# The seven passages between sub-layers: a panel's split in four pieces, and the first chunk's high part made by VectorE from the scaled stream

## Chip, cores and metric

One Trainium2 chip, one core, one launch. The metric is the time of the launch on the device in microseconds, lower is better. TensorE (PE), VectorE (DVE), ScalarE (ACT), GpSimd (POOL) and SyncE's DMA queue (SP) run their own instruction streams and wait for each other through semaphores.

## What is computed

272 tokens (16 meta tokens and 256) of width 1024 pass through eight sub-layers: FFN, neighbourhood attention, FFN, FFN, differential attention, FFN, a mixer of block attention and mLSTM, and an MLP. Each is

```
h = h + c * rmsnorm(f(rmsnorm(h, g_in)), g_post)      # f: projections, attention, swiglu or relu^2
rmsnorm(x, g) = x * rsqrt(mean(x*x) + 1e-6) * g
```

From the fifth sub-layer on, 256 tokens are carried. All weights are fp32.

## The kernel before

**Layout.** The stream `h` lies in SBUF with the width on the partitions: 8 chunks `h[:, c, :]` of 128 rows by 272 (later 256) tokens. Sub-layer k (0 to 7) is phases n = 2k (into it) and 2k+1 (out of it). `NA, DA, MIX, MLP` are k = 1, 4, 6, 7.

**Split products.** Every fp32 product is made of three: high by high, high by low, low by high. A panel of weights, 1024 rows by 256 columns (128x2048 in SBUF), comes by DMA into `raw`, ACT rounds it to `w_hi` (`high`, L1400), DVE makes `w_lo = raw - w_hi` (`low`, L1856). Four slots are used in turn. The activations are split in the same way: ACT makes `x_hi[c] = h[c] * gain[c]` (`high_part`, L1463), DVE `x_lo[c]` (`low_part`, L1867). The factor rsqrt of the norm is not in them. It is applied to the products later, so that they need not wait for it.

**A passage** is the way from sub-layer k to k+1, k = 0 to 6. What stands below as passage k is this:

1. `last_panel`: PE makes the two halves (m = 0, 1) of the last output bank one after the other; ACT squares each (`square_half`, L1429).
2. `sum_rest`: PE sums the squares over the partitions with matmuls against ones: L925 (earlier squares), at k = 0, 2, 3, 5 L928 (half 0), and L932 (half 1). Then eight small matmuls by `keep_warm` (L941) fill PE's time. At k = 1, 4, 6 half 0 has been added by DVE before, and L928 is left out.
3. `deviation`: ACT makes `sd` (L1443) and `floor` (L1446) from the sum. The stream is carried scaled: with it `h*sd + y` is the new stream, where `y` are the scaled outputs (`scaled_y`, L1890).
4. `residual`: DVE, chunk by chunk: `scale_h` (L1896, h*sd), `add_y` (L1902, + y), and between them `low_part`. ACT makes `x_hi` of each chunk when it is added.
5. `first_panels`: PE takes the first two panels of the next phase together, chunk by chunk (`shared_chunk`): 8 matmuls with `x_hi` of the chunk (L709), then 4 with `x_lo` (L715). It waits for each chunk's `x_hi` and `x_lo`.

At k = 0, 2, 3, 5 (after an FFN) both panels' `low` stand on DVE's stream ahead of `residual`, and both panels' `high` on ACT's stream ahead of the square of half 0. At k = 1, 4, 6 the same holds, with smaller phases before them. GpSimd adds squares of the output (L2702, L2707) and has nothing to do in the passage itself.

The orders of all engines are written out by hand; no planner is used.

Of the kernel before, what the change touches and what calls it, by code (L numbers as in the profile page):

```python
# [135 lines left out]
def program(nc, A, out):  # L136

    with ExitStack() as ctx:
# [34 lines left out]
        ones = sb("ones", [P, P])  # L173
        eps = sb("eps", [P, 2])
# [61 lines left out]
        c = [end]  # L236
        line = sb("line", [8, 2 * NT - 1 - NM], F32, c)
        assert c[0] <= nc.sbuf_usable_end
# [78 lines left out]
        w_lo_ready = sem("w_lo_ready")  # L317
        panel_used = sem("panel_used")
# [10 lines left out]
        sum_ready = sem("sum_ready")  # L329
        sd_ready = sem("sd_ready")  # L330
# [171 lines left out]
        def mixer_count(k):  # L502

            return (NA, DA, MIX).index(k)
# [20 lines left out]
        def _(sp):  # L525
# [50 lines left out]
            def between(n, panel):  # L576
# [4 lines left out]
                if n == 5:  # L581

                    if panel == 0:
                        sp.wait_ge(line_full, 16)
                        sp.wait_ge(h_ready, DC * (NA + 2))
                    if panel < 8:
                        da_bias_in(panel)
                if n == 11 and panel == 0:

                    sp.wait_ge(h_ready, DC * (DA + 2))  # L590
                    for dst, src in ((causal[:, :], A["causal"]), (causal_t[:, :], A["causal_t"]),
                                     (rotate[:, :], A["rotate"]), (pick[:, :], A["pick"]), (freq[:, :], A["freq"]),
                                     (pos_i[:, :], A["positions_2"][0].partition_broadcast(P)),
                                     (tail[:, :, :], rows(A["w_in_2"][0])[:, :, 3072:3080])):
                        sp.dma_start(dst, src).then_inc(mix_full, 16)

            for n, ph in enumerate(PHASES):
                bodies = ph.panels // 4
                first = 0
                if n == 2 * MLP + 1:  # L600
                    sp.wait_ge(h_ready, DC * (MIX + 2))
# [42 lines left out]
        def _(pe):  # L644
# [44 lines left out]
            def first_panels(k_, tokens):  # L689
# [3 lines left out]
                for k in range(DC):  # L693
                    shared_chunk(n, SPLIT_IN[k_], tokens, k)

            def shared_chunk(n, base, tokens, k):

                    ph = PHASES[n]
                    pe.wait_ge(x_hi_ready, base + k + 1)
                    for j in range(2):  # L700
                        if k == 0:
                            pe.wait_ge(w_lo_ready, ph.p0 + j + 1)
# [3 lines left out]
                        for m in range(2):  # L706
                            w = slice(k * CW + m * P, k * CW + m * P + P)
                            for part in (w_hi, w_lo):
                                nc.tensor.matmul(banks(n, 0, j)[:, m, 0:tokens], part[:, (ph.p0 + j) % SLOTS, w],  # L709
                                                 x_hi[:, k, 0:tokens], start=k == 0 and part is w_hi, stop=False)  # L710
                    pe.wait_ge(x_ready, base + k + 1)
# [207 lines left out]
            def sum_rest(k_, tokens):  # L919

                if k_ in (NA, DA, MIX):
                    pe.wait_ge(post_summed, mixer_count(k_) + 1)
                pe.wait_ge(sq_added, additions(2 * k_ + 1) + 3)
                pe.wait_ge(sd_ready, 2 * k_ + 1)
                nc.tensor.matmul(ps_post[:, 0:tokens], ones[:, :], sq_sum[:, 0, 0:tokens], start=True, stop=False)  # L925
                if k_ not in (NA, DA, MIX):
                    pe.wait_ge(sq_ready, squares_before(2 * k_ + 1) + 4)
                    nc.tensor.matmul(ps_post[:, 0:tokens], ones[:, :], sq[:, 1, 0, 0:tokens], start=False, stop=False)  # L928
# [5 lines left out]
                if k_ < MLP:  # L934
                    keep_warm(aux[:, 0, :], 8)
# [452 lines left out]
        def _(act):  # L1388
# [70 lines left out]
            def high_part(k, c):  # L1459

                g0, _, _, tokens, _ = SUBS[k]
                act.wait_ge(h_ready, DC * k + c + 1)
# [13 lines left out]

            def boundary(k):

                tokens = SUBS[k][4]
                square_half(k, 0)  # L1480
                square_half(k, 1)
                deviation(k, tokens)
                n = 2 * k + 2
# [28 lines left out]
            def output_steps(n, k):  # L1512
# [5 lines left out]
                def step(i, j):  # L1518
# [10 lines left out]
                    if local == last - 2 and k < MLP:  # L1529
                        high(n, i, j + 3)  # L1530
                        if k not in (NA, DA, MIX):
                            high(n, i, j + 4)
# [313 lines left out]
        def _(dve):  # L1846
# [51 lines left out]
            def add_y(k, c0, c1):  # L1898

                tokens = SUBS[k][4]  # L1900
                dve.wait_ge(scaled_ready, DC * k + c1)
                nc.vector.tensor_tensor(h[:, c0:c1, 0:tokens], h[:, c0:c1, 0:tokens], y[:, c0:c1, 0:tokens], ALU.add)\  # L1902
                    .then_inc(h_ready, c1 - c0)

            def residual(k):


                tokens = SUBS[k][4]
                for m in range(2):
                    dve.wait_ge(sq_ready, squares_before(2 * k + 1) + 4 + m)  # L1910
                    ins = scaled_y(k, 6 + m, out_bank(k, 1)[:, m, 0:tokens], tokens)
                ins.then_inc(acc_free, 1)
                dve.wait_ge(sd_ready, 2 * k + 2)
                scale_h(k, 0, 1)
                add_y(k, 0, 1)
                scale_h(k, 1, 2)
                add_y(k, 1, 2)
                if k < MLP:
                    low_part(k + 1, 0)
                for q in range(1, 4):  # L1920
                    scale_h(k, 2 * q, 2 * q + 2)
                    if k < MLP and q > 1:
                        low_part(k + 1, 2 * q - 2)
# [3 lines left out]
                    if k < MLP:  # L1927
                        low_part(k + 1, 2 * q - 1)
                if k == MLP:
                    return  # L1930
# [92 lines left out]
            def output_steps(n, k):  # L2023
# [6 lines left out]
                def step(i, j):  # L2030
# [14 lines left out]
                    if local == last - 2 and k < MLP:  # L2045
                        low(n, i, j + 3)
                        if k not in (NA, DA, MIX):
                            low(n, i, j + 4)
                    if local == last - 1 and k in (NA, DA, MIX):
                        dve.wait_ge(sq_ready, squares_before(2 * k + 1) + 4)  # L2050
                        dve.wait_ge(sq_added, additions(2 * k + 1) + 3)
                        nc.vector.tensor_tensor(sq_sum[:, 0, 0:tokens], sq_sum[:, 0, 0:tokens], sq[:, 1, 0, 0:tokens],
                                                ALU.add).then_inc(post_summed, 1)
                        low(n, i, j + 3)
                    if k == 0 and local in (4, 6, 9, 11):
# [641 lines left out]
        def _(pool):  # L2697
# [11 lines left out]

            for k in range(8):  # L2710
# [43 lines left out]
                if k < MLP:  # L2754
                    add_squares(2 * k + 1, SUBS[k][4], k not in (NA, DA, MIX))

# [61 lines left out]
```

## Time and profile before

| | |
|---|---|
| time, median of 3 runs (lowest to highest) | 1434.78 us (1433.89 to 1434.93) |
| the profiled execution: its span, first to last instruction | 1436.0 us |
| PE busy | 1419.0 us, 99% |
| DVE busy | 947.8 us, 66% |
| ACT busy | 662.0 us, 46% |
| POOL busy | 45.6 us, 3% |
| mean granted TensorE clock | 0.998 |

Shares of busy time are means over the whole span. The profiled execution has no time of its own beside its span, which is 1.2 us (0.09%) above the median of the runs. PE's busy time includes the matmuls of `keep_warm`, which compute nothing.

### The profile page before, as it was taken

The page shows a single profiled execution, that of the slowest core. Times are in us where ns is not written, and L with a number is a line of the kernel's source. Part 1 is how long each engine was busy: PE and PEld are TensorE (multiplying, and loading weights), DVE is VectorE, ACT ScalarE, POOL GpSimd, SP SyncE. Part 2 cuts the span into 40 slices and gives each one's busy share as a digit, 9 for nine tenths or more (in the row PEclk, how much of TensorE's full clock was granted, in tenths as well). Part 3 has the DMA queues.
Part 4 walks back from the last instruction along what each step waited for, and adds up shares of the span by engine and source line. Part 5 has one row for each costly group of instructions (what it writes and reads, how often), then busy time and mean ns, then how long its engine had stood idle before and what let it go on. Part 6 is the DMA issues. An engine that isn't in the chain of part 4 may idle for free.

```text
span 1436.0 us, 26258 instructions
## 1 busy us (share of the span) xinstructions
PE 1419.0 (99%) x10988; PEld 1361.9 (95%) x10988; DVE 947.8 (66%) x1223; ACT 662.0 (46%) x876; POOL 45.6 (3%) x72
## 2 busy tenths in 40 slices
PE   9999999999999999999999999999999999999998
PEld 9999999978999999999999988999999997999887
DVE  6656568566865555866557677876656975787653
ACT  5444345544544343544435357544444555544432
POOL 0000010010000000000001000000001010000000
PEclk9999999999999999999999999999999999999999
DMA  7586765511455576455454640465656540356552
GB/s 219 177 226 186 206 195 161 176 61 60 147 176 175 173 217 200 147 176 175 145 168 157 205 147 2 146 206 176 191 175 205 172 152 30 119 176 208 187 195 99
DMA packets 238904, 233.99 MB, mean 163 GB/s; under 512 B 29791, under 2 KB 233492, under 8 KB 238816
## 3 DMA queue, kind: packets, MB, share of 16 engines
q1 hardware_dynamic: 238024, 232.33, 52.4%
q8 instruction: 66, 1.08, 0.3%
q10 hardware_dynamic: 792, 0.40, 0.1%
q14 instruction: 22, 0.18, 0.0%
HBM read 231.52 MB, written 1.12 MB: 162 GB/s over the span
## 4 chain that ended last, share of the span: by engine, by line
PE 92%; DVE 3%; ACT 2%; DMA 2%; issue 1%; DVEq 0%; SPq 0%; ACTq 0%
PE acc L646 22%; PE acc L647 22%; PE acc L648 22%; PE acc L709 4%; PE aux L876 2%; PE aux L875 2%; PE aux L874 2%; PE acc L715 2%; PE aux L646 2%; PE aux L647 2%; PE aux L648 2%; PE aux L941 1%; PE acc L1154 1%; ACT w_hi L1400 1%; PE acc L1262 1%
## 5 line engine op out<-in xcount | busy, mean ns | idle before, releaser
L646 PE MATMUL acc<-x_hi,w_hi 128*128 128x272 f32 (+1 forms) x1960 | 559.8, 286 | 1.6 <-DVE z L1999 0.9
L647 PE MATMUL acc<-x_lo,w_hi 128*128 128x272 f32 (+1 forms) x1960 | 559.6, 286 | 0.0
L1856 DVE TENSOR_TENSOR w_lo<-raw,w_hi 128x2048 fp32r<-128x2048 f32 (+1 forms) x229 | 482.0, 2109 | 117.3 <-ACT w_hi L1400 116.6
L648 PE MATMUL acc<-x_hi,w_lo 128*128 128x272 f32 (+1 forms) x1960 | 557.9, 285 | 0.0
L1400 ACT ACTIVATE w_hi<-raw 128x2048 fp32r<-128x2048 f32 (+3 forms) x251 | 407.0, 1627 | 171.1 <-DMA raw<-in_ffn_w_down 52.7
L646 PEld LDWEIGHTS acc<-x_hi,w_hi 128*128 128x128 f32 x1960 | 369.4, 188 | 4.5 <-issue 1.7
L647 PEld LDWEIGHTS acc<-x_lo,w_hi 128*128 128x128 f32 x1960 | 368.2, 188 | 0.3 <-issue 0.2
L648 PEld LDWEIGHTS acc<-x_hi,w_lo 128*128 128x128 f32 x1960 | 368.3, 188 | 0.0
L646 PE MATMUL acc<-hid_hi,w_hi 128*128 128x272 f32 (+1 forms) x704 | 201.9, 287 | 0.0
L647 PE MATMUL acc<-hid_lo,w_hi 128*128 128x272 f32 (+1 forms) x704 | 201.6, 286 | 0.0
L648 PE MATMUL acc<-hid_hi,w_lo 128*128 128x272 f32 (+1 forms) x704 | 200.7, 285 | 0.0
L1999 DVE TENSOR_TENSOR z<-acc,rstd 128x544 f32<-128x544 f32 (+1 forms) x95 | 67.2, 712 | 136.0 <-PE acc L648 135.8
L1828 ACT ACTIVATE hid_hi<-z 128x544 f32 (+3 forms) x44 | 28.7, 652 | 248.5 <-DVE z L2663 246.4
L648 PEld LDWEIGHTS acc<-hid_hi,w_lo 128*128 128x128 f32 x704 | 132.6, 188 | 0.0
L647 PEld LDWEIGHTS acc<-hid_lo,w_hi 128*128 128x128 f32 x704 | 132.6, 188 | 0.0
L646 PEld LDWEIGHTS acc<-hid_hi,w_hi 128*128 128x128 f32 x704 | 132.4, 188 | 0.1
L709 PE MATMUL acc<-x_hi,w_hi 128*128 128x272 f32 (+1 forms) x256 | 66.2, 289 | 4.7 <-ACT x_hi L1463 4.7
L709 PE MATMUL acc<-x_hi,w_lo 128*128 128x272 f32 (+1 forms) x256 | 64.9, 284 | 0.0
L646 PE MATMUL aux<-x_hi,w_hi 128*128 128x272 f32 (+1 forms) x200 | 59.0, 295 | 1.9 <-DVE w_lo L1856 1.9
L2666 DVE TENSOR_TENSOR hid_lo<-z,hid_hi 128x544 f32 (+3 forms) x44 | 31.6, 718 | 40.3 <-ACT hid_hi L1828 40.3
L647 PE MATMUL aux<-x_lo,w_hi 128*128 128x272 f32 (+1 forms) x200 | 57.7, 288 | 0.0
L648 PE MATMUL aux<-x_hi,w_lo 128*128 128x272 f32 (+1 forms) x200 | 57.6, 288 | 0.0
(340 smaller groups left out, 1610.5 us busy)
## 6 DMA issues: line engine op xcount, KB each, us to landing
raw<-in_ffn_w_gate SPq DMA_DIRECT2D x44, 1024.0 KB, 5.4
raw<-in_ffn_w_up SPq DMA_DIRECT2D x44, 1024.0 KB, 5.4
raw<-in_ffn_w_down SPq DMA_DIRECT2D x32, 768.0 KB, 4.9
raw<-in_ffn_w_down SPq DMA_DIRECT2D x32, 640.0 KB, 4.4
raw<-in_w_up SPq DMA_DIRECT2D x16, 1024.0 KB, 5.4
raw<-in_w_down SPq DMA_DIRECT2D x16, 1024.0 KB, 4.8
raw<-in_na_w_qkv SPq DMA_DIRECT2D x12, 1024.0 KB, 5.2
raw<-in_da_w_qkv SPq DMA_DIRECT2D x12, 1024.0 KB, 5.3
```

Source lines behind the costliest of these rows:

```text
L646: nc.tensor.matmul(o, wh, xh, start=first, stop=False)
L647: nc.tensor.matmul(o, wh, xl, start=False, stop=False)
L648: return nc.tensor.matmul(o, wl, xh, start=False, stop=last)
L709: nc.tensor.matmul(banks(n, 0, j)[:, m, 0:tokens], part[:, (ph.p0 + j) % SLOTS, w], x_hi[:, k, 0:tokens], start=k == 0 and part is w_hi, s ...
L715: mm = nc.tensor.matmul(banks(n, 0, j)[:, m, 0:tokens], w_hi[:, (ph.p0 + j) % SLOTS, w], x_lo[:, k, 0:tokens], start=False, stop=k == DC - 1)
L874: nc.tensor.matmul(o, mlp_hi[:, k, tok], w_hi[:, slot, w], start=first, stop=False)
L875: nc.tensor.matmul(o, mlp_hi[:, k, tok], w_lo[:, slot, w], start=False, stop=False)
L876: return nc.tensor.matmul(o, mlp_lo[:, k, tok], w_hi[:, slot, w], start=False, stop=last)
L1400: ins = nc.scalar.activation(w_hi[:, slot, w], raw[:, slot, w], ACT.Copy)
L1856: nc.vector.tensor_tensor(w_lo[:, slot, w], raw[:, slot, w], w_hi[:, slot, w].bitcast(F32), ALU.subtract)\
L1999: ins = nc.vector.tensor_tensor(dst, src, spread(0, tokens), ALU.mult)
L2666: nc.vector.tensor_tensor(hid_lo[:, dst, 0:tokens], up, hid_hi[:, dst, 0:tokens].bitcast(F32), ALU.subtract).then_inc(hid_ready, 1)
```

## The change

At passages k = 0, 2, 3, 5 the second panel of the next phase is split in four pieces of 128x512. ACT's pieces (`high_piece`) stand around the squares of the last bank and around `deviation`, DVE's (`low_piece`) two inside `residual` before `sd` is waited for and two between the chunks. PE waits for the pieces two chunks at a time. `post_sum` (DVE adds half 0's squares) takes the place of L928 here too.

At all seven passages the first chunk goes another way. In the step before `residual` DVE makes `y_first = y[0]*gain` (`first_gain`). After `sd` it makes `h_first = h[0]*sd` and straight from it `x_hi[0] = h_first*gain + y_first`. GpSimd makes the true sum `h[0] = h_first + y[0]` (`add_first`), which `low_part` 0 and the squares of the first pair of chunks wait for. PE takes the high matmuls of chunks 0 and 1 first, then their low ones. `keep_warm` at the end of `sum_rest` is cut from eight to six matmuls. `line`, a table of the start, is laid over `y` to make room for the two new tiles.

```diff
         def first_panels(k_, tokens):
-                for k in range(DC):
+                for k in (0, 1):
+                    shared_high(n, SPLIT_IN[k_], tokens, k)
+                for k in (0, 1):
+                    shared_low(n, SPLIT_IN[k_], tokens, k)
+                for k in range(2, DC):
                     shared_chunk(n, SPLIT_IN[k_], tokens, k)
...
+            def shared_high(n, base, tokens, k):
                     ph = PHASES[n]
                     pe.wait_ge(x_hi_ready, base + k + 1)
                     for j in range(2):
+                        in_pieces = n % 2 == 0 and j == 1 and n // 2 - 1 not in (NA, DA, MIX)
+                        if in_pieces and k % 2 == 0:
+                            if k < 6:
+                                pe.wait_ge(lo_piece, pieces_before(n // 2 - 1) + k // 2 + 1)
+                            else:
+                                pe.wait_ge(w_lo_ready, ph.p0 + 2)
...
             def sum_rest(k_, tokens):
-                if k_ in (NA, DA, MIX):
-                    pe.wait_ge(post_summed, mixer_count(k_) + 1)
-                pe.wait_ge(sq_added, additions(2 * k_ + 1) + 3)
+                pe.wait_ge(post_summed, k_ + 1)
...
-                if k_ not in (NA, DA, MIX):
-                    pe.wait_ge(sq_ready, squares_before(2 * k_ + 1) + 4)
-                    nc.tensor.matmul(ps_post[:, 0:tokens], ones[:, :], sq[:, 1, 0, 0:tokens], start=False, stop=False)
...
-                    keep_warm(aux[:, 0, :], 8)
+                    keep_warm(aux[:, 0, :], 6)
...
             def boundary(k):
                 square_half(k, 0)
+                if in_pieces:
+                    high_piece(n, 0)
+                    high_piece(n, 1)
                 square_half(k, 1)
+                if in_pieces:
+                    high_piece(n, 2)
                 deviation(k, tokens)
-                for c in range(DC):
+                if in_pieces:
+                    high_piece(n, 3)
+                for c in range(1, DC):
                     high_part(k + 1, c)
                     if c % 2:
                         high(n, 0, 2, c // 2, 4)
+                        act.wait_ge(first_added, k + 1)
                         square(n, c // 2, h[:, c - 1:c + 1, 0:tokens], tokens)
...
+            def first_gain(k):
+                dve.wait_ge(acc_free, PHASES[2 * k + 1].a0 + 1)
+                nc.vector.tensor_scalar(y_first[:, 0:tokens], y[:, 0, 0:tokens], gains[:, g0:g0 + 1], None, ALU.mult)
...
+            def first_chunk(k, tokens):
+                dve.wait_ge(sd_ready, 2 * k + 2)
+                nc.vector.tensor_tensor(h_first[:, 0:tokens], h[:, 0, 0:tokens], sd[:, 0:tokens], ALU.mult).then_inc(first_scaled, 1)
+                dve.wait_ge(first_scaled, k + 1)
+                nc.vector.scalar_tensor_tensor(out=x_hi[:, 0, 0:tokens], in0=h_first[:, 0:tokens], scalar=gains[:, g0:g0 + 1],
+                                               in1=y_first[:, 0:tokens], op0=ALU.mult, op1=ALU.add).then_inc(x_hi_ready, 1)
...
             def residual(k):
+                if in_pieces:
+                    post_sum(k)
                 for m in range(2):
                     dve.wait_ge(sq_ready, squares_before(2 * k + 1) + 4 + m)
                     ins = scaled_y(k, 6 + m, out_bank(k, 1)[:, m, 0:tokens], tokens)
+                    if in_pieces and m == 0:
+                        low_piece(2 * k + 2, 0)
+                        low_piece(2 * k + 2, 1)
                 ins.then_inc(acc_free, 1)
-                dve.wait_ge(sd_ready, 2 * k + 2)
-                scale_h(k, 0, 1)
-                add_y(k, 0, 1)
+                first_chunk(k, tokens)
                 scale_h(k, 1, 2)
                 add_y(k, 1, 2)
-                if k < MLP:
-                    low_part(k + 1, 0)
                 for q in range(1, 4):
                     scale_h(k, 2 * q, 2 * q + 2)
-                    if k < MLP and q > 1:
-                        low_part(k + 1, 2 * q - 2)
+                    if q == 1:
+                        dve.wait_ge(first_added, k + 1)
+                    low_part(k + 1, 2 * q - 2)
                     if q == 3:
                         dve.wait_ge(acc_free, PHASES[2 * k + 1].a0 + 4)
                     add_y(k, 2 * q, 2 * q + 2)
+                    if in_pieces and q < 3:
+                        low_piece(2 * k + 2, q + 1)
+                    low_part(k + 1, 2 * q - 1)
...
+            def add_first(k, tokens):
+                pool.wait_ge(first_scaled, k + 1)
+                nc.gpsimd.tensor_tensor(h[:, 0, 0:tokens], h_first[:, 0:tokens], y[:, 0, 0:tokens], ALU.add)\
+                    .then_inc(first_added, 1)
```

## Rows read from the trace of the kernel before

**Rows 1.** Page, part 1: busy us, share of the span, instructions.

```profile
PE 1419.0 (99%) x10988; PEld 1361.9 (95%) x10988; DVE 947.8 (66%) x1223; ACT 662.0 (46%) x876; POOL 45.6 (3%) x72
```

**Rows 2.** Waits of PE: waiter, releaser, us in total, times, longest.

```profile
PE acc L709 <- ACT x_hi L1463: 4.7, 7, 1.3
```

**Rows 3.** Timeline of PE, passages 0, 1, 2, 3, 5: start, us, instruction.

```profile
215.75 0.62 PE L925 MATMUL aux<-sq_sum,ones 128*128 128x272 f32 x2
...
220.47 0.67 PE L715 MATMUL acc<-x_lo,w_hi 128*128 128x272 f32 x4
...
365.42 0.62 PE L925 MATMUL aux<-sq_sum,ones 128*128 128x272 f32 x2
...
567.96 0.62 PE L925 MATMUL aux<-sq_sum,ones 128*128 128x272 f32 x2
...
772.59 0.62 PE L925 MATMUL aux<-sq_sum,ones 128*128 128x272 f32 x2
...
1105.27 0.60 PE L925 MATMUL aux<-sq_sum,ones 128*128 128x256 f32 x2
```

**Rows 4.** Chain that ended last, in order of time: start, us, what.

```profile
219.37 1.26 PE acc L709 x8
...
368.97 1.28 PE acc L709 x8
...
567.02 1.92 ACT w_hi L1400
568.96 2.29 DVE w_lo L1856
...
573.51 1.27 PE acc L709 x8
...
777.03 1.26 PE acc L709 x8
...
1109.96 1.22 PE acc L709 x8
```

**Rows 5.** Timeline of ACT, passages 0 (first row) and 1.

```profile
215.94 0.40 ACT L1429 ACTIVATE sq<-acc 128x272 f32<-128x272 f32 x1 [0.87 <-PE acc L648]
...
365.62 0.49 ACT L1429 ACTIVATE sq<-acc,gains 128x272 f32<-128x272 f32 x1 [2.54 <-PE acc L648]
366.93 0.49 ACT L1443 ACTIVATE sd<-aux,eps 128x272 f32<-128x272 f32 x1 [0.82 <-PE aux L932]
...
368.40 0.52 ACT L1463 ACTIVATE x_hi<-h,gains 128x272 fp32r<-128x272 f32 x1 [0.61 <-DVE h L1902]
```

**Rows 6.** Timeline of DVE, passage 1.

```profile
367.45 0.44 DVE L1896 TENSOR_TENSOR h<-h,sd 128x272 f32<-128x272 f32 x1 [0.74 <-ACT sd L1443]
367.92 0.44 DVE L1902 TENSOR_TENSOR h<-h,y 128x272 f32<-128x272 f32 x1
...
369.11 0.50 DVE L1867 SCALAR_TENSOR_TENSOR x_lo<-h,gains,x_hi 128x272 fp32r<-128x272 f32 x1
369.53 0.72 DVE L1896 TENSOR_TENSOR h<-h,sd 128x544 f32<-128x544 f32 x1
370.35 0.73 DVE L1902 TENSOR_TENSOR h<-h,y 128x544 f32<-128x544 f32 x1
370.99 0.50 DVE L1867 SCALAR_TENSOR_TENSOR x_lo<-h,gains,x_hi 128x272 fp32r<-128x272 f32 x1
```

**Rows 7.** Timeline inside k = 4, where one DVE instruction releases DVE and POOL.

```profile
884.51 0.42 DVE L2568 TENSOR_TENSOR o_rows<-o_rows,stat 128x256 f32<-128x256 f32 x1
884.56 0.85 POOL L2729 TENSOR_TENSOR o_rows<-o_rows,stat 128x256 f32<-128x256 f32 x1 [109.20 <-DVE stat L2561]
...
884.86 0.83 DVE L2568 TENSOR_TENSOR o_rows<-o_rows,stat 128x256 f32<-128x256 f32 x1
...
886.70 0.61 POOL L2729 TENSOR_TENSOR o_rows<-o_rows,stat 128x256 f32<-128x256 f32 x1
```

**Rows 8.** Timeline in the FFN of k = 2, DVE and POOL.

```profile
553.78 1.90 POOL L2707 TENSOR_TENSOR sq_sum<-sq_sum 128x272 f32<-128x272 f32 x1
...
554.97 2.33 DVE L1856 TENSOR_TENSOR w_lo<-raw,w_hi 128x1536 fp32r<-128x1536 f32 x1
```

More of the change, by code:

```diff
@@ L173, in program @@
         ones = sb("ones", [P, P])
+        y_first = sb("y_first", [P, NT])
+        h_first = sb("h_first", [P, NT])
         eps = sb("eps", [P, 2])
@@ L235, in program @@
         assert c[0] <= z_at
-        c = [end]
+        c = [y_at]
         line = sb("line", [8, 2 * NT - 1 - NM], F32, c)
-        assert c[0] <= nc.sbuf_usable_end
         c = [region]
@@ L710, in shared_chunk, with shared_low @@
                                                  x_hi[:, k, 0:tokens], start=k == 0 and part is w_hi, stop=False)
+            def shared_low(n, base, tokens, k):
+                    ph = PHASES[n]
                     pe.wait_ge(x_ready, base + k + 1)
@@ L1475, in split_first, with high_piece @@
                     square(0, pair, h[:, 2 * pair:2 * pair + 2, 0:tokens], tokens)
+            def high_piece(n, piece):
+                ph = PHASES[n]
+                slot = (ph.p0 + 1) % SLOTS
+                size = FULL * CW // 4
+                w = slice(piece * size, piece * size + size)
+                if piece == 0:
+                    act.wait_ge(raw_full[slot], ((ph.p0 + 1) // 4 + 1) * 16)
+                nc.scalar.activation(w_hi[:, slot, w], raw[:, slot, w], ACT.Copy)\
+                    .then_inc(hi_piece if piece < 3 else w_hi_ready, 1)
             def boundary(k):
                 tokens = SUBS[k][4]
+                n = 2 * k + 2
+                in_pieces = k not in (NA, DA, MIX)
                 square_half(k, 0)
+                if in_pieces:
+                    high_piece(n, 0)
+                    high_piece(n, 1)
                 square_half(k, 1)
+                if in_pieces:
+                    high_piece(n, 2)
                 deviation(k, tokens)
-                n = 2 * k + 2
-                for c in range(DC):
+                if in_pieces:
+                    high_piece(n, 3)
+                for c in range(1, DC):
                     high_part(k + 1, c)
@@ L2046, in step @@
                         low(n, i, j + 3)
-                        if k not in (NA, DA, MIX):
-                            low(n, i, j + 4)
                     if local == last - 1 and k in (NA, DA, MIX):
[L2050 to L2053, printed above, removed]
+                        post_sum(k)
                         low(n, i, j + 3)
+                    if local == last - 1 and k < MLP:
+                        first_gain(k)
                     if k == 0 and local in (4, 6, 9, 11):
@@ L2755, in _ @@
                     add_squares(2 * k + 1, SUBS[k][4], k not in (NA, DA, MIX))
+                    add_first(k, SUBS[k][4])
 def t5_buckets():
```

53 lines of the change are left out of this document (39 added, 14 removed).

## Prediction

> **What bounds the kernel now.** I read the page first. PE is busy 99% of the span [rows 1]; the change takes no product away, so it can win only time in which PE does nothing that counts. The view of waits then shows that PE waits little: the largest entry is for the first chunk's `x_hi`, seven times, once per passage, 4.7 us in all [rows 2]. That is too small a measure, because the matmuls of `keep_warm` fill most of each passage and count as busy. So I took a length that they can't hide: from the start of L925, where the last useful product has just been issued (T0), to the first L709 of the next phase. The timeline of PE gives the first, the chain that ended last the second [rows 3, 4]:
>
> passage 0: 219.37 - 215.75 = 3.62; passage 1: 368.97 - 365.42 = 3.55; passage 2: 573.51 - 567.96 = 5.55; passage 3: 777.03 - 772.59 = 4.44; passage 5: 1109.96 - 1105.27 = 4.69. Passages 4 and 6 are built like 1, with 256 tokens.
>
> The reader is to see that 2, 3 and 5 are 0.8 to 1.9 us longer than 0 and 1. The chain of passage 2 says why: `w_hi` of the second panel starts at 567.02, `w_lo` follows at 568.96 and takes 2.29 us, and `residual` stands behind it on DVE [rows 4]. In 0 and 1 the chain goes through `sd` instead. About 29 us lie in the seven passages.
>
> **The pieces and the dropped matmul: the way to `sd`.** What would passages 0, 2, 3, 5 take if neither DVE nor ACT were late? Passage 1 shows it, since L928 is missing there: the square of half 1 starts at T0 + 0.20 and takes 0.49, `sd` ends at 367.42 = T0 + 2.00 [rows 3, 5]. In the FFN passages the square takes 0.40, 0.09 less [rows 5], so `sd` ends at T0 + 1.91; call that end E. Can the pieces keep up? A piece on DVE has 512 columns; the nearest row is the same kind of instruction on 544, 0.72 long, its follower 0.64 after its start [rows 6]; I take 0.61. In passage 2, the worst, ACT can start its pieces at 567.0 (T0 - 0.9, when its `w_hi` starts now), and two of them are done by 568.15, just when half 1 is ready to be squared (T0 + 0.20). Each is a quarter of 1.92, with a start of its own some 0.55 to 0.6. DVE has `post_sum` (0.44) and one `scaled_y` before that, the two pieces until 568.9, the second `scaled_y` until 569.4, and E is 569.87. It holds with 0.5 us to spare. In passage 3 `w_lo` of the first panel ends late and `first_gain` stands behind it, and I count 0.08 for that. The other two pieces on ACT lie in its waits for `sd` and for chunk 1. `first_gain` costs nothing elsewhere: DVE sat idle for 0.74 before `sd` in passage 1 [rows 6], and the step is shorter than the 0.50 of the nearest row; without that cover it would be 0.4 a passage. Six instead of eight warming matmuls cost and give nothing, as long as they end before the first L709.
>
> **The first chunk.** Now, from E: `scale_h` at 0.03, `add_y` 0.47 later, ACT's `x_hi` 0.48 after that, 0.52 long, PE 0.05 after its end: E + 1.55 [rows 4 to 6]. After: `h_first` at 0.03, the direct `x_hi` at 0.50, a SCALAR_TENSOR_TENSOR of 0.50, PE at E + 1.05.
> First L709 after T0: 3.05 in passage 1 and 1.91 + 1.05 = 2.96 in the FFN ones. Won: 0.66 (0), 0.50 (1), 2.59 (2), 1.40 (3), 1.73 (5), and 0.50 each for 4 and 6. **Sum won: 7.9 us.**
>
> **What PE meets next.** Starting the first chunk earlier does not bring the second. PE's eight high matmuls take 1.10 (220.47 - 219.37) [rows 3, 4], so PE asks for `x_hi` of chunk 1 at E + 2.15. DVE comes to `scale_h` of chunk 1 at E + 0.92. Undisturbed that gives `add_y` at 1.39, ACT from 1.87 to 2.39 and PE at 2.44: 0.29 idle. Chunk 1 does not gain, because DVE's two steps on chunk 0 are as long as before.
>
> But GpSimd's sum now runs exactly there. It is released by `h_first`, as DVE's own next step is. Such a pair is in the trace: DVE's step starts 0.05 before POOL's and takes its normal 0.42; POOL's takes 0.85, against 0.61 for the same instruction later alone; and DVE's next one takes 0.83 instead of 0.42 [rows 7]. They take turns, and the step that is stopped is the one behind. In the new code that is `scale_h` of chunk 1. The price: 0.41 for a POOL step of 0.61. For a POOL step with two full tensors of 272, which `add_first` is, the FFN shows `w_lo` of 1536 columns at 2.33 [rows 8], where 1536/2048 of 2.29 is 1.72: 0.6. Ends: 0 (if they did not meet) and 0.85, POOL's whole step in [rows 7]; I take 0.60, the row of the same form. Should GpSimd get in first, `x_hi` 0 is late by as much, `scale_h` of chunk 1 comes out at the same time, and the sum hardly changes.
>
> The Trainium skill ("SBUF — State Buffer", section "Who interferes with whom") states this against the change: a VectorE instruction with two SBUF inputs and a GpSimd instruction that reads SBUF exclude each other, for the whole instruction, in order of issue. The trace agrees in kind. By the rule's whole instruction, the sum would be about 1 us higher than by my 0.60.
>
> With 0.60, chunk 1's `x_hi` lets PE go on at E + 3.04: 0.89 idle, and 0.10 for a start from rest (1.10 for eight matmuls that follow each other by 0.127, [rows 3]).
>
> Then chunk 1's low part. After `add_y` of chunk 1 (1.99) DVE does `scale_h` 2-3 (2.35), `low_part` 0 (2.99), `add_y` 2-3 (3.41), at an FFN passage a piece (4.05), and `low_part` 1 (4.66 to 5.16), by the steps of [rows 6] (0.64, 0.42, 0.64, and 0.61 for the piece). PE has done chunk 1 high and chunk 0 low at 3.04 + 1.11 + 0.51 = 4.66 and waits until 5.21: 0.55, and 0.10 again. At passages 1, 4, 6 there is no piece, `low_part` 1 ends at 4.55, PE waits for nothing. From there DVE needs 0.64 + 0.42 + 0.64 + 0.61 + 0.42 = 2.73 for two chunks, PE 3.0, so PE waits no more. What follows (`w_lo` of the third and fourth panel, the sums of squares, the reciprocal, the first evictions) moves later on DVE by about 1.6 us and PE by the same; I count nothing.
>
> **Sum lost:** FFN passages 0.89 + 0.10 + 0.55 + 0.10 = 1.64, four times 6.56; the others 0.99, three times 2.97: **9.5 us**. Against 7.9 won: +1.6 us on a span of 1436.0, and the same on the median 1434.78: **1436.4 us**, +0.11%. A measurement of this kernel can tell about 0.2%, 2.9 us, from no change, so this is no change.
>
> **Rivals.**
> *A. GpSimd's sum does not hold VectorE back.* For: the timeline shows it for other operands than these. Against: every case in which both read SBUF at once shows it [rows 7, 8]. PE would idle 0.39 instead of 0.99 in each passage and 0.65 more at the FFN ones, as above: 4 x 1.04 + 3 x 0.39 = 5.3 lost, 7.9 won, -2.6 us: 1432.2, just short of 0.2%. Chance 0.15, half of it past the bound.
> *B. The stop is longer (the other side).* If `scale_h` of chunk 1 stands for 0.85, seven times 0.25 is added: +3.4, 1438.2. It decides from 0.78 on ((2.9 - 1.6)/7 = 0.18 above 0.60). For: POOL's first step takes 0.85 and L2707 is shown with 1.90 [rows 7, 8]. Against: 1.90 began while DVE's `w_lo` before it still ran until 555.0, so 1.2 of it is POOL's own wait, and DVE's own loss there is 0.6. The page's rule gives +2.6 here and belongs on the near side of the bound. Chance 0.15. If the 1.90 were GpSimd's work, it would be some 9 us; 0.02.
> *C. The change does not bring the earlier `sd`.* The second panel lands late in passage 2, and the pieces push the square of half 1 back; then 2.59, 1.40 and 1.73 shrink by about 0.6 each: +3.4, 1438.2. Against: ACT's 567.02 leaves room, if barely. Chance 0.05.
> *D. More is won than I count* (for instance `low_part` 1 is not waited for): -1.5 to -4. Chance 0.08.
> Forecast: 0.55.
>
> **Numbers.** Faster 0.14 (half of A, most of D). Slower 0.22 (B with its tail, C). Same 0.64. The range takes in A and the 0.85 of B: 1431.9 to 1438.3. The forecast's own is 1435.0 to 1437.7.
>
> **What will show it.** First L709 about 3.0 us after L925 in all passages, with `x_hi` 0 from DVE in the chain. `scale_h` of chunk 1 at about 1.0 us instead of 0.44, and POOL's sum at 0.7 to 1.3. PE waits for ACT's `x_hi` of chunk 1 seven times about 0.9, and for `x_lo` of chunk 1 four times about 0.55. If `scale_h` of chunk 1 is 0.44, A holds; if the first L709 is later than T0 + 3.3 at 2, 3 or 5, C does. A wait in the third or fourth panel of the next phase, or a granted clock below full in a passage, would make the sum wrong.

## The result

| kernel | median, us (lowest to highest, runs) | ratio, 95% interval |
|---|---|---|
| before | 1434.86 (1433.89 to 1437.78, 6) | |
| after | 1444.73 (1442.48 to 1456.27, 6) | 1.0075 [1.0055, 1.0095] |

The change makes the kernel slower by 0.75%, 9.9 us. I had predicted 1436.4 us, no change, and at most 1438.3. One of the 91 executions of before that were timed beside the experiments took 2308.64 us at a mean clock of 0.555; it stands in no median and in no table below. The page of the profiled execution of after, which is the slowest of the six (1456.27), answers to [rows 1]:

```profile
span 1454.3 us, 26247 instructions
...
PE 1434.2 (99%) x10952; PEld 1369.6 (94%) x10952; DVE 956.5 (66%) x1246; ACT 659.6 (45%) x881; POOL 49.3 (3%) x79
...
PEclk9999999999999999999999999999999995999999
```

The last line is the granted clock in 40 slices. One slice, around 1220 us, is at half. Read in windows of 4 us (window, length, busy us and instructions of PE, PEld, DVE, ACT, POOL, then the clock), after:

```profile
1196.00:1200.00 4.00, 4.00 (x26) 3.21 (x26) 2.93 (x10) 2.46 (x10) 0.00 (x0) 1.00 0.00 0
1200.00:1204.00 4.00, 3.55 (x21) 2.76 (x20) 1.99 (x7) 2.25 (x11) 0.00 (x0) 0.92 0.00 0
1204.00:1208.00 4.00, 4.00 (x13) 2.69 (x12) 2.24 (x6) 1.36 (x5) 0.00 (x0) 0.50 0.00 0
...
1232.00:1236.00 4.00, 4.00 (x18) 3.49 (x18) 1.04 (x3) 1.03 (x4) 0.00 (x0) 0.50 0.00 0
1236.00:1240.00 4.00, 4.00 (x31) 4.00 (x30) 2.64 (x7) 1.19 (x3) 0.00 (x0) 0.81 0.00 0
```

and before, at the same place:

```profile
1200.00:1204.00 4.00, 3.96 (x23) 2.86 (x23) 2.16 (x6) 2.21 (x8) 0.00 (x0) 1.00 0.00 0
1204.00:1208.00 4.00, 3.96 (x23) 2.85 (x22) 2.67 (x10) 1.56 (x8) 0.00 (x0) 1.00 0.01 4
```

For some 34 us (the shares of the windows below 1.00 added up) the clock is 1.2 instead of 2.4 GHz. This is inside sub-layer 6, between passages 5 and 6, where neither kernel has work that the other lacks. From L925 of passage 5 (in after it is L953) to that of passage 6 lie 142.2 us in before and 156.7 in after: 14.5 of the 18.3 us between the two profiles are this one fall.

The rest is in the view of PE's waits (waiter, releaser, us in all, times, longest), which answers to [rows 2]:

```profile
PE acc L735 <- DVE x_hi L1982: 5.7, 7, 0.9
PE aux L656 <- DVE w_lo L1899: 1.9, 1, 1.9
PE acc L745 <- DVE x_lo L1910: 1.6, 4, 0.5
PE acc L656 <- DVE z L2081: 1.5, 2, 0.9
```

L735 is the old L709, L745 the old L715. The second row is in before too; `z` is there in before once, with 0.9. The table has, for each passage, the time from T0 (start of L925, now L953) to the first high matmul and to the end of the shared panels' block, from the timelines of PE:

| passage | before: first | block | after: first | block | block, after - before |
|---|---|---|---|---|---|
| 0 | 3.62 | 15.98 | 3.56 | 16.88 | +0.90 |
| 1 | 3.55 | 15.91 | 3.66 | 16.38 | +0.47 |
| 2 | 5.55 | 17.91 | 3.56 | 16.88 | -1.03 |
| 3 | 4.44 | 16.82 | 3.56 | 16.88 | +0.06 |
| 4 | 3.42 | 15.07 | 3.51 | 15.50 | +0.43 |
| 5 | 4.69 | 16.30 | 3.45 | 16.15 | -0.15 |
| 6 | 3.35 | 15.00 | 3.44 | 15.39 | +0.39 |

The sum is +1.07 us, near the 1.6 that I had worked out, though by other steps. So the passages of the two profiles don't hold the loss, and this is what the experiments had to explain.

Passage 1 of after, DVE first, then POOL, then PE (answering to [rows 3, 6]):

```profile
368.61 0.44 DVE L1980 TENSOR_TENSOR h_first<-h,sd 128x272 f32<-128x272 f32 x1 [0.47 <-ACT sd L1468]
369.09 1.10 DVE L1982 SCALAR_TENSOR_TENSOR x_hi<-h_first,gains,y_first 128x272 fp32r<-128x272 f32 x1
370.11 0.43 DVE L1939 TENSOR_TENSOR h<-h,sd 128x272 f32<-128x272 f32 x1
```

```profile
369.13 0.76 POOL L2792 TENSOR_TENSOR h<-h_first,y 128x272 f32<-128x272 f32 x1 [12.08 <-DVE h_first L1980]
```

```profile
370.24 0.40 PE L735 MATMUL acc<-x_hi,w_hi 128*128 128x272 f32 x1 [0.85 <-DVE x_hi L1982]
...
371.22 0.29 PE L735 MATMUL acc<-x_hi,w_lo 128*128 128x272 f32 x1
371.63 0.40 PE L735 MATMUL acc<-x_hi,w_hi 128*128 128x272 f32 x1
```

The reader is to see 1.10 on the direct `x_hi`, where I had 0.50, and 0.43 on `scale_h` of chunk 1, where I had 1.0: GpSimd gets in first. The first chunk's high part comes 0.1 us later after T0 than in before (3.66 against 3.55), and PE still waits about 0.3 for the second.

### The profile page after: what moved, and what is told of

The parts are those of the page before. It is cut to its first block, busy times and chain, and to the rows that moved or that the text cites. A ratio compares the mean times of both kernels' runs of the same rounds, so it can differ in the third digit from the quotient of the medians.

```text
span 1454.3 us, 26247 instructions
## 1 busy us (share of the span) xinstructions
PE 1434.2 (99%) x10952; PEld 1369.6 (94%) x10952; DVE 956.5 (66%) x1246; ACT 659.6 (45%) x881; POOL 49.3 (3%) x79
## 4 chain that ended last, share of the span: by engine, by line
PE 91%; DVE 5%; ACT 2%; issue 2%; DMA 0%; DVEq 0%; SPq 0%; ACTq 0%
PE acc L656 22%; PE acc L657 22%; PE acc L658 22%; PE acc L735 3%; PE aux L906 2%; PE aux L904 2%; PE aux L905 2%; PE aux L966 2%; PE acc L745 1%; PE aux L656 1%; PE aux L657 1%; PE aux L658 1%; PE acc L1179 1%; PE acc L1287 1%; ACT w_hi L1425 1%
## 5 line engine op out<-in xcount | busy, mean ns | idle before, releaser
L1899 DVE TENSOR_TENSOR w_lo<-raw,w_hi 128x2048 fp32r<-128x2048 f32 (+2 forms) x225 | 473.1, 2107 | 110.7 <-ACT w_hi L1425 110.1
L1425 ACT ACTIVATE w_hi<-raw 128x2048 fp32r<-128x2048 f32 (+3 forms) x247 | 399.4, 1622 | 158.8 <-DMA raw<-in_ffn_w_down 51.6
L735 PE MATMUL acc<-x_hi,w_hi 128*128 128x272 f32 (+1 forms) x256 | 67.0, 293 | 6.6 <-DVE x_hi L1982 5.7
L735 PE MATMUL acc<-x_hi,w_lo 128*128 128x272 f32 (+1 forms) x256 | 64.9, 284 | 0.0
```

What stands on the lines that cost most here:

```text
L1425: ins = nc.scalar.activation(w_hi[:, slot, w], raw[:, slot, w], ACT.Copy)
L1899: nc.vector.tensor_tensor(w_lo[:, slot, w], raw[:, slot, w], w_hi[:, slot, w].bitcast(F32), ALU.subtract)\
```

## Experiments

The runs came in four groups (`again`, `place`, `nopool`, `pieces`; `before_again`, `first`, `mixwarm`, `later`; `short`, `before_third`, `first8`; `place_short`), each on one chip with before beside it. Since the granted clock of an execution varies, I read each result a second time by it. The table gives medians (runs) over all executions with that mean granted clock; before is from the first three groups with `before_again`. Beside `place_short` before has 1434.78 at 1.000 (5), so the groups can be set side by side. An equal clock leaves out what a change itself does to the clock; the section on why the prediction was wrong comes back to that.

| granted clock | 1.000 | 0.999 | 0.998 | 0.997 | 0.996 |
|---|---|---|---|---|---|
| before | 1434.82 (28) | 1436.75 (5) | 1437.13 (8) | 1437.38 (13) | 1439.34 (23) |
| again | 1442.18 (2) | | 1442.99 (2) | | 1445.76 (2) |
| place | 1440.19 (2) | 1440.81 (2) | 1440.69 (1) | 1441.07 (1) | 1443.26 (1) |
| pieces | 1436.25 (1) | 1437.72 (1) | | 1438.03 (6) | 1440.22 (2) |
| later | 1434.28 (2) | | 1436.43 (1) | 1436.89 (3) | 1439.01 (5) |
| short | 1433.28 (3) | 1433.76 (9) | | | |
| place_short | 1440.38 (1) | | | | 1443.69 (2) |

**The changed kernel once more**, unchanged.

> The changed kernel once more, for a second profile. Its first one has 33 us in the mixer (k = 6) at a granted clock of 0.50, which cost 14.6 us of its 18.3 over the profile of before. Theory 1 (the fall is an event that comes in some executions): this profile shows it in another place or length, or not at all; without it the span is about 1440 to 1441, and the passages, from L925 to the end of the shared panels, still add up to about +1.1 us against before, the row products of the MLP to +1.7. Theory 2 (the fall belongs to the change, at a fixed place): 33 us at 0.50 again, near 1204 us.

Measured: 1443.0 us (1442.13 to 1445.9, 6 runs), before 1436.82, ratio 1.0045 [1.003, 1.006]. The profiled span is 1441.3 at clock 0.998: 13 us less than the first one, with the passages the same to 0.05 us, and the fall in sub-layer 6 is 6.8 us long instead of 34. So about a third of the first measurement's loss lies in executions with longer falls: at clock 0.998 the first measurement has 1442.48 and 1443.24, this one 1442.99. At an equal clock 5.9 to 7.4 us remain.

**The two new tiles behind everything else.**

```diff
-        y_first = sb("y_first", [P, NT])
-        h_first = sb("h_first", [P, NT])
...
+        c = [end]
+        y_first = sb("y_first", [P, NT], F32, c)
+        h_first = sb("h_first", [P, NT], F32, c)
```

> The changed kernel with y_first and h_first behind the large region, where line lay, instead of ahead of it, so that every other tile has its address of before. Theory 1 (the 2176 bytes by which mlp_hi and mlp_lo moved make the 384 row products of the MLP slower, 396 ns instead of 388 to 394): L904 to L906 are back at 388 to 394 ns, the stretch from the end of passage 6 to the end is 173.5 us instead of 175.2, and the time is 1.7 us below the changed kernel. Rival (their rate differs from execution to execution): as long as the changed kernel, 396 ns in some profiles whatever the address.

Measured: 1441.07 (1440.12 to 1449.03, 11), ratio 1.0041 [1.0024, 1.0057]; at an equal clock about 2 us under `again`. The groups by form of the MLP's row products show why (mean ns stands behind the bar and the busy time), before (from 1262.5 us to 1424), `again` and `place` (both from 1270 to 1425; over the whole span each group has 128 matmuls):

```profile
L876 PE MATMUL aux<-w_hi,mlp_lo 128*128 128x512 f32 x120 | 47.3, 394 | 0.0
L875 PE MATMUL aux<-w_lo,mlp_hi 128*128 128x512 f32 x120 | 47.0, 392 | 0.0
L874 PE MATMUL aux<-w_hi,mlp_hi 128*128 128x512 f32 x120 | 46.6, 388 | 0.0
```

```profile
L904 PE MATMUL aux<-w_hi,mlp_hi 128*128 128x512 f32 x115 | 45.5, 395 | 0.0
L906 PE MATMUL aux<-w_hi,mlp_lo 128*128 128x512 f32 x114 | 45.1, 396 | 0.0
L905 PE MATMUL aux<-w_lo,mlp_hi 128*128 128x512 f32 x114 | 45.1, 395 | 0.0
```

```profile
L907 PE MATMUL aux<-w_lo,mlp_hi 128*128 128x512 f32 x112 | 43.9, 392 | 0.0
L908 PE MATMUL aux<-w_hi,mlp_lo 128*128 128x512 f32 x111 | 43.7, 394 | 0.0
L906 PE MATMUL aux<-w_hi,mlp_hi 128*128 128x512 f32 x112 | 43.5, 388 | 0.0
```

The two tiles stand ahead of others in SBUF and move all that follow by 2176 bytes. By these rows the 384 products are 2 to 7 ns longer each in `again`, and the stretch from the end of passage 6's block to the end of the span is 175.2 us instead of 173.5; in `place` it is 173.6. The same 175.2 stands in after and `nopool`, and 173.5 to 173.6 in every profile in which the two tiles lie behind everything or are absent.

**The true sum on VectorE**, after `scale_h` of chunks 2 and 3, instead of on GpSimd.

```diff
-                    add_first(k, SUBS[k][4])
...
                     if q == 1:
+                        nc.vector.tensor_tensor(h[:, 0, 0:tokens], h_first[:, 0:tokens], y[:, 0, 0:tokens], ALU.add)\
+                            .then_inc(first_added, 1)
                         dve.wait_ge(first_added, k + 1)
```

> The changed kernel with the true sum h[0] = h_first + y[0] made by VectorE, just before low_part 0, instead of by GpSimd. Theory 1 (GpSimd's sum holds the direct x_hi for 0.60): the direct x_hi takes 0.50 instead of 1.10, the first L735 comes 0.60 earlier, at T0 + 3.0, chunk 1's x_hi 0.60 earlier too; low_part 1 comes 0.60 - 0.4 = 0.2 earlier. The passages end 0.2 to 0.6 us earlier each, some 2.5 us in all. Rival (the direct x_hi takes 1.10 by itself, as an instruction with two tensors and a per-partition gain into x_hi): it stays at 1.10 and the time rises by the added 0.4 us per passage, up to 2.8 us. If the excess over before is mostly a lower clock, the time stays 5 us or more above before in both cases.

Measured: 1443.45 (1441.34 to 1444.22, 6), ratio 1.0038 [1.0024, 1.0052]; at clock 0.999 it has 1441.38. Passage 1 on DVE and PE:

```profile
368.38 0.44 DVE L1980 TENSOR_TENSOR h_first<-h,sd 128x272 f32<-128x272 f32 x1 [0.48 <-ACT sd L1468]
368.85 0.50 DVE L1982 SCALAR_TENSOR_TENSOR x_hi<-h_first,gains,y_first 128x272 fp32r<-128x272 f32 x1
```

```profile
369.41 0.40 PE L735 MATMUL acc<-x_hi,w_hi 128*128 128x272 f32 x1 [0.26 <-DVE x_hi L1982]
```

Without GpSimd the direct `x_hi` takes 0.50 and PE starts 0.6 us earlier in every passage, at T0 + 2.88 to 3.06: my E + 1.05. But the blocks end only 0.05 to 0.2 us earlier (16.76, 16.25, 16.78, 16.75, 15.36, 15.95, 15.33). The waits tell where it went:

```profile
PE acc L745 <- DVE x_lo L1910: 4.0, 7, 0.9
...
PE acc L735 <- DVE x_hi L1982: 1.6, 7, 0.3
```

The 0.6 us move from the first chunk to `x_lo` of the first chunks, which wait for the same DVE work as before. What limits the block here is DVE's sum of steps, not when the first chunk is there. The run does not show what the earlier chunk would give by itself, since it also puts the sum, a step of 0.4 us, on DVE.

**The four pieces alone**, with the first chunk as in before.

```diff
-                for c in range(1, DC):
+                for c in range(DC):
                     high_part(k + 1, c)
...
-                first_chunk(k, tokens)
+                dve.wait_ge(sd_ready, 2 * k + 2)
+                scale_h(k, 0, 1)
+                add_y(k, 0, 1)
                 scale_h(k, 1, 2)
                 add_y(k, 1, 2)
+                low_part(k + 1, 0)
```

> The kernel before with the four pieces and post_sum at the four FFN passages alone: first chunk by ScalarE as before, eight warming matmuls, no new tiles, no GpSimd sum. By the steps of the prediction sd ends at T0 + 1.9 and the first L709 comes at T0 + 3.5 at all of them: 0.1, 2.1, 0.9 and 1.2 earlier than before, 4.3 us in all; chunk 1's low part waits up to 0.3 behind a piece. Theory 1 (the loss sits in the first chunk's new way): 3 to 4 us faster than before, and no fall of the clock. Theory 2 (the pieces themselves bring the loss): as slow as the changed kernel.

> The kernel before, unchanged, for a second profile and the granted clock of each of its executions. Theory 1 (the fall in the mixer near 1200 us comes also in the kernel before, in some executions): some executions at a mean clock of 0.997 or less, and the spread of its times (1434.3 to 1439.7 in 22 runs) follows the clock. Theory 2 (it belongs to the changed kernels alone): all executions at 0.998 or more. Second question: its first profile is 1436.0 with 1.5 us of it lost near 904 us at a lower clock. If its executions at clock 1.000 have a span of 1432.5, another 2 us lie in something that this profile shows, such as the start of passage 2 (5.55 us), which waited for a DMA.

Measured: `pieces` 1438.22 (1436.25 to 1449.21, 12), ratio 1.0021 [1.0005, 1.0038]; `before_again` 1437.46 (12), ratio 1.0008 [0.9998, 1.0019]. By the profiles `pieces` should win: its blocks end at 16.43, 15.91, 16.41, 16.41, 15.07, 15.57, 15.01 after T0, 2.2 us less in all than in before. It doesn't: at an equal clock it is 0.7 to 1.4 us slower. The profile of `before_again` has its first high matmul at 6.23, 4.17 and 4.44 after T0 at passages 2, 3 and 5, where before had 5.55, 4.44 and 4.69 [rows 3, 4]. Loads are late there in every profile of before, but by amounts that vary. The row of the chain that stands ahead of `w_hi` in passage 2 is the load of the second panel (start, us), in before, `before_again` and `before_third`:

```profile
559.88 7.11 DMA raw<-in_ffn_w_up
```

```profile
559.61 7.79 DMA raw<-in_ffn_w_up
```

```profile
560.95 7.62 DMA raw<-in_ffn_w_up
```

`w_hi` follows it at T0 - 0.94, T0 - 0.26 and T0 - 0.44. My 5.7 us won at these three were read from one execution.

**The first chunk's way alone**, tiles as in `place`, both panels whole; then the same with eight warming matmuls.

```diff
-                in_pieces = k not in (NA, DA, MIX)
+                in_pieces = False
```

```diff
-                    keep_warm(aux[:, 0, :], 6)
+                    keep_warm(aux[:, 0, :], 8)
```

> The kernel before with the first chunk's new way alone, at all seven passages (GpSimd's sum, high matmuls of chunks 0 and 1 first, six warming matmuls; the new tiles behind the region): no pieces, and the matmul for half 0's squares as before. By the measured passages of the changed kernel, the first high matmul comes 0.1 later than before and the shared panels end 0.45 later at each passage: +3.1 us at the same clock. Rival (the first chunk's way costs nothing by itself, the excess comes from the pieces): within 1 us of before.

> The run first with eight warming matmuls at the end of sum_rest, as in before, instead of six. In first the clock fell in passages 2 and 3 (576 and 782 us) as well. Theory 1 (the two warming matmuls taken away make the falls in the passages): no fall there, the clock of all executions at 0.995 or more, median some 5 to 10 us below first, and at clock 1.000 the same 1439.5 to 1440. Rival (the longer wait for the direct x_hi makes them, 2 us and more from the last warming matmul on): the same falls, median within 2 us of first.

Measured: `first` 1449.89 (1440.16 to 1453.33, 6), ratio 1.0073 [1.0046, 1.01]; `first8` 1442.62 (1441.1 to 1448.35, 10), 1.0046 [1.0031, 1.0061]. At clock 0.999 they have 1440.16 and 1441.1, one execution each, where before has 1436.75: the way alone costs some 3.4 to 4.4 us. A wait and two windows of `first`, inside the shared panels of passages 2 and 3:

```profile
PE acc L737 <- DVE x_hi L1991: 9.3, 7, 2.1
```

```profile
576.00:580.00 4.00, 4.00 (x21) 4.00 (x22) 4.00 (x8) 3.81 (x9) 0.00 (x0) 0.60 0.00 0
780.00:784.00 4.00, 3.67 (x17) 3.67 (x18) 3.96 (x9) 2.77 (x6) 1.09 (x2) 0.57 0.01 2
```

Six warming matmuls do not fill the passage when a load is late: PE stands 2.02 us before L737 in passage 2, and the clock falls behind it. With eight the fall at 780 is gone and the one at 576 stays, so neither of the two theories of `first8` holds in full. In the changed kernel's profiles, where the first high matmul comes at 3.44 to 3.66, the clock falls in no passage.

**More warming inside sub-layer 6.** To `place` two `keep_warm` matmuls are added at each step of the attention loop of sub-layer 6.

```diff
-                        if step % 3 == 1 or step > 11:
+                        if step > 0:
                             keep_warm(aux[:, step % 2, 3 * P:], 2)
```

> The kernel of the run place with two more warming matmuls at each step of the mixer's attention loop (k = 6) that had none, so that TensorE is given more to do there. Theory 1 (the clock falls there because TensorE's work is thin, and the change only moved the kernel to where the falls come more often): no stretch at 0.50 near 1200 us, all executions at 0.998 or more, 3 to 5 us off the median of place, less what the added matmuls cost where TensorE is not waiting (up to 2 us). Rival (the falls come whatever TensorE does there): the same falls, and up to 2 us slower.

Measured: 1443.5 (1442.25 to 1444.57, 5), ratio 1.0044 [1.0031, 1.0058]. In its profile the windows that stood at 0.50 are at 1.00:

```profile
1200.00:1204.00 4.00, 4.00 (x27) 3.26 (x25) 3.55 (x8) 1.94 (x10) 0.00 (x0) 1.00 0.00 0
1204.00:1208.00 4.00, 4.00 (x25) 3.00 (x24) 1.53 (x7) 1.84 (x8) 0.00 (x0) 1.00 0.00 0
```

All its executions have 0.998 or more, but the added matmuls cost much of what the fall does: 129.18 us from the end of passage 5's block to T0 of passage 6, against 125.9 in before and 130.77 in `place`, which has a fall of 10.2 us. In passage 3 a load that took 7.85 us also pushed the square back (a wait of 0.8), and the first high matmul came at T0 + 4.34: my rival C, once. So the pieces do not take every late load out.

**The last two pieces behind the low parts** of chunks 1 and 3, in `pieces`.

```diff
-                    if in_pieces and q < 3:
-                        low_piece(2 * k + 2, q + 1)
                     low_part(k + 1, 2 * q - 1)
+                    if in_pieces and q < 3:
+                        low_piece(2 * k + 2, q + 1)
```

> The run pieces with the third and fourth pieces of w_lo behind low_part 1 and low_part 3 instead of ahead of them. In pieces TensorE waits 0.4 for x_lo of chunk 1 at each of the four FFN passages (0.5 with the start from rest). Theory: this wait goes, the third piece is ready at about E + 4.7 and is needed at E + 4.6 to 5.1, so at most 0.1 comes back: 1.6 to 2 us below pieces. Rival (something behind it is late next): chunk 2's x_hi or the pieces are waited for instead, and the time stays.

Measured: 1438.02 (1434.09 to 1444.05, 12), ratio 1.0006 [0.9993, 1.002]; 0.3 to 0.7 us under before at an equal clock, 1.1 to 2.0 under `pieces`. The 0.45 us that `x_lo` of chunk 1 waits for a piece are real and go with the order. This is the best of the changed kernels, and it is no change. A part of its gain comes back where PE waits for `z` in the next phase:

```profile
PE acc L654 <- DVE z L2076: 2.3, 2, 1.3
PE acc L729 <- ACT x_hi L1482: 1.9, 7, 0.3
```

**Late loads taken out of before.** The loads of the first two panels behind passages 2, 3 and 5 are shortened to a quarter, so six panels are not the reference's weights.

```diff
+                if phase_index in (6, 8, 12) and isinstance(i, int) and i == 0 and j < 2:
+                    sp.dma_start(raw[:, slot, 0:2 * CW].rearrange("p (k n) -> p k n", n=width),
+                                 source(phase_index, i, j)[:, 0:2, :]).then_inc(raw_full[slot], 16)
```

> The kernel before with the loads of the first two panels after passages 2, 3 and 5 cut to a quarter of their bytes, so that they can't land late. ScalarE reads that quarter four times over and VectorE subtracts w_hi from itself for w_lo, with the lengths of before; the weights of six panels are therefore not the reference's. In the trace the first high matmul comes at T0 + 3.6 at passages 2, 3 and 5 instead of 5.6 to 6.2, 4.2 to 4.4 and 4.4 to 4.7, about 4 us less in all. Theory 1 (both profiles of before show loads later than most of its executions have them): at an equal clock less than 1.5 us faster than before, and at clock 1.000 about 1434. Theory 2 (the loads are as late in the timed executions): 3.5 to 4 us faster at an equal clock, 1431 at clock 1.000; then what the pieces win is lost again somewhere that I have not found.

> The kernel before, unchanged, for a third profile: whether the first high matmul of passages 2, 3 and 5 comes at T0 + 5.6 to 6.2, 4.2 to 4.4 and 4.4 to 4.7 again (theory 2 of the run short) or sooner (theory 1), and whether its clock falls near 904 us and near 1200 us.

Measured: 1433.63 (1432.9 to 1434.77, 12), ratio 0.9972 [0.9962, 0.9982]. Its first high matmuls come at 3.61, 3.62 and 3.48 after T0. The profiles of before (this is the third) lie 4.0, 4.1 and 3.7 us above it at these three passages together. But the timed executions lie only 1.5 us above it at clock 1.000, and 3.0 at 0.999. So an execution of before at full clock seems to lose less to late loads than any of its three profiles shows. Two things stand against taking 1.5 for the whole effect. By the medians the shorter loads give 3.8 us (1437.42 to 1433.63), because none of the twelve executions of `short` has a clock under 0.999, while 52 of before's 90 have (the one at 0.555 left out). And the profile of `short` has a fall behind passage 3 (124.5 us up to T0 of passage 4, against 122.9 without one) at a time of 1433.43, yet its executions at 1.000 take 1433.28 and not 1431.9: some 1.4 us of them are in no profile.

**The same loads shortened in the changed kernel** (in `place`; here too six panels are not the reference's weights).

> This is `place` (the changed kernel with its two new tiles behind the region) with the loads of `short`: the first two panels that follow passages 2, 3 and 5 are cut to a quarter of their bytes, and both parts of these six panels are made from that quarter, so their weights are not the reference's. All steps and products keep their sizes. My account of the loss so far: at equal granted clock `place` is 4 to 5.4 us above the kernel before, and its profiled passages are only 1.1 us longer than before in all, because the profile of before holds 3.8 us of late loads at passages 2, 3 and 5 that its other executions hold only in part. Theory 1 (the pieces take the late loads out, so the changed kernel has none to lose): cutting the loads gives `place` nothing, 1440 at clock 1.000, 0 to 0.5 below `place`, and the block of shared panels ends at the same distances after L925 as in `place` (16.91, 16.89, 16.15). Against `short` (1433.28 at clock 1.000) it is then about 6.5 above, 5.1 of it in the seven passages and 0.6 at the wait for z. Theory 2 (the changed kernel has late loads of its own in executions that no profile shows, and they are part of its loss): it comes out at least 1.5 us below `place` at an equal clock, 1438.7 or less at 1.000.

Measured: 1444.62 (1440.38 to 1449.63, 7), ratio 1.0054 [1.0035, 1.0073]. At clock 1.000 it has 1440.38 against 1440.19 of `place`, at 0.995 three executions with 1444.62 to 1444.88 against 1444.8. Its blocks end at 16.89, 16.38, 16.88, 16.89, 15.46, 16.14, 15.39: to 0.04 us those of `place`. In these executions the changed kernel has no late loads to lose. With the loads out of both, it is 7.1 us slower (one execution against three), where the profiles show 5.0 in the passages and 0.6 at `z`.

## Why the prediction was wrong

**The profiled execution was not a typical one.** I set its span beside the median (1436.0 against 1434.78) and called them 1.2 apart. The later results list span and time of each execution: for before the time is 1.74 to 1.94 above the span. So the profiled one had a time of about 1437.8, 3.0 above the median. It had a fall of the clock at 900 to 908 us, worth 1.6 us (124.5 instead of 122.9 in the stretch after passage 3), and the late loads. The median execution, by its time, had neither in full (its clock is not on record), and a gain that consists in taking them away is not there to be had on the median.

**The profile's late loads were taken for a constant.** This is the step that failed first: "Won: 0.66 (0), 0.50 (1), 2.59 (2), 1.40 (3), 1.73 (5)". 3.8 of the 5.7 us at passages 2, 3 and 5 are the amounts by which [rows 3, 4] exceed passage 0 in one execution. In timed ones at clock 1.000, where by its time the measured median of before lies (1434.86 against 1434.82), shortening the loads gives 1.5. The pieces do what the change says, 3.44 to 3.57 in all FFN passages, but there is less to win: 2.3 us of the error. `short` and `place_short` point to it from both sides, by three executions and one at 1.000. `pieces` and `later` agree: their profiles without the falls are 1.1 and 2.4 us shorter than that of before without its fall, while their executions at 1.000 are 1.4 longer and 0.5 shorter.

**The first chunk won nothing.** I took 0.50 for the direct `x_hi`; it took 1.10 at 272 tokens and 1.05 at 256, in all seven passages. I had named this case ("Should GpSimd get in first ...") and had said that the sum hardly changes. That was right: `nopool` gives the 0.6 back at the first matmul and little of it at the block's end. The terms inside were wrong (idle 0.89 before chunk 1; measured about 0.9 before chunk 0 and 0.3 before chunk 1), the seven passages together +1.07 where I had +1.6. The stop of a GpSimd step of two full tensors was 0.60, my value; rival A fell in all seven passages, and B too.

The Trainium skill ("SBUF — State Buffer", section "Who interferes with whom") says that the two exclude each other for the whole instruction, in order of issue. The trace agrees that one waits for the other. By their recorded starts, 369.09 and 369.13, the later one went first here, and the price was 0.60 of POOL's 0.76, so order and size are the measurement's.

**The pieces between the chunks.** `x_lo` of chunk 1 waited 0.4 to 0.5 four times, where I had 0.55. Right.

**"What follows ... moves later on DVE by about 1.6 us and PE by the same; I count nothing."** Wrong by 0.57: at the fourth panel behind passage 2, `z` is late (before doesn't wait there at all; it has one wait for `z`, after has two).

**The two tiles.** I had no term for where they lie. 1.7 us in the profiles, about 2 in the timed runs; `place` shows it.

**The clock.** I had looked for it only in passages and put nothing for it elsewhere. It never fell in a passage in the profiles of the changed kernel. It fell in sub-layer 6, for 6.8 to 34 us, and this is the largest part of the miss: the first measurement's loss is 3.7 us above the second's (9.9 against 6.2), mostly by that. It isn't the change's alone: the third profile of before has a fall of 6.8 us there as well, and before has executions at 0.996, 4.5 us above those at 1.000. But the longer falls come with the change. At 0.995 or less are 3 of the changed kernel's twelve timed executions (0.986, 0.992, 0.994), 8 of the 18 of `place` and `place_short`, 7 of the 16 of `first` and `first8`, 3 of the 24 of `pieces` and `later`, and none of before's 90 (the one at 0.555 left out). Why they are longer is not shown; `mixwarm` shows only that more matmuls in sub-layer 6 go with none.

The account for `again`: 1.07 + 2.3 + 0.57 + 1.7 = 5.6 us, against 6.2 by the medians and 7.4 at clock 1.000. With `place_short` and `short` it is 5.7 against 7.1. So up to 1.8 us stay open; they don't hang on the loads, and since 0.004 of mean clock goes with 4.5 us in before, a clock rounded to 0.001 leaves about 0.6 us of it uncertain. For the forecast itself: 8.3 us were missing between 1.6 and 9.9. Of these 3.7 are the clock, 2.3 the loads, 1.7 the place of the tiles and 0.6 `z`; the passages took 0.5 less than I had counted, and 0.5 stays open.

## What to carry to other kernels

A gap that a late transfer makes is a sample from one execution: before a gain is built on it, look at several profiles, or shorten the transfer and time that. Making the first of a chain of chunks earlier won next to nothing here, because the engine that makes all of them was as busy as the consumer; the sum of its steps up to each chunk decided, so moving work off it counts only if the other engine doesn't stop it. New buffers are better put behind all others, so that nothing else moves. And a median taken at one clock cannot be set against one at another: read both at an equal clock, and say beside it what the change does to the clock.

## What the hardware showed that I had not expected

- Moving `mlp_hi` and `mlp_lo` by 2176 bytes in SBUF made the mean of 128x512 matmuls 395 to 396 ns instead of 388 to 394 (`again`), and putting them back undid it (`place`).
- Where one DVE instruction released both DVE and POOL, POOL's step started 0.04 us behind DVE's and, by the durations, was served first in all seven passages (DVE 1.10 instead of 0.50, or 1.05 instead of 0.48 at 256 tokens). At 884.5 [rows 7] the start differs by 0.05 in the same direction, and DVE is served first.
- In a stretch of sub-layer 6 with 21 to 28 matmuls in 4 us, after a gap of 0.45 us, the granted clock goes to 0.50 and stays there for 6.8, 10.2, 20.5 or 34 us (windows added up) in the profiles of `again`, `place`, `first` and after, for nearly the same instructions. The same gap stands in the profiles of before and `short`, which have no fall there, so the gap by itself does not bring it. With two more small matmuls at each step the profile has 1.00 there.
